# The order of three partial products: low weights last in the dense tiles of a two-block layer, and its first two tiles interleaved

## The reference, cut to what matters

```python
# block one
proj = h @ w_in + b_in                       # 512 x 1024 @ 1024 x 8208
y_a  = spatial_gating(gelu(u), gelu(v))      # u, v: columns of proj
y_b  = gated_delta_rule(silu(conv(qkv)), ...) * silu(z)
merged = sigmoid(gate_a) * (y_a @ w_pa) + sigmoid(gate_b) * (y_b @ w_pb)
h = layer_norm(ALPHA * h + merged @ w_o)
h = layer_norm(ALPHA * h + mixture_of_experts(h))
# block two: input projection (v, k, q, a, x, r, s), attention, recurrence, output projection, feed-forward
```

## Time and profile before

| | us |
|---|---|
| median of 3 runs (lowest, highest) | 2144.96 (2140.62, 2145.87) |
| the profiled execution, its time | 2142.25 |
| the profiled execution, its span | 2140.4 |
| TensorE busy with matmuls | 1981.0 (93% of the span), 9702 matmuls |
| VectorE busy | 926.3 (43%) |
| ScalarE busy | 660.6 (31%) |
| GpSimd busy | 434.7 (20%) |
| TensorE's mean granted clock | 0.969 |

### The profile page before, as it was taken

How to read it: one execution, slowest core, us unless ns; L and a number is a source line. 1 busy time by engine, 2 the same in 40 slices (tenths; PEclk the granted TensorE clock), 3 DMA queues, 4 the chain that set the end, 5 groups by cost and what they waited for, 6 DMA issues and landing times.

```text
span 2140.4 us, 23345 instructions
## 1 busy us (share of the span) xinstructions
PE 1981.0 (93%) x9702; PEld 1447.1 (68%) x9702; DVE 926.3 (43%) x1402; ACT 660.6 (31%) x981; POOL 434.7 (20%) x310
## 2 busy tenths in 40 slices
PE   7999999999999889888788799998889999999999
PEld 6887878888877733333333348777667787888887
DVE  7774376632535622111111145445545883222342
ACT  4554332423333101000000133452137753222221
POOL 5432131423326011111111021311003210000121
PEclk9999999999999889989899999999999999999999
DMA  5861433123244589999999973211111134323210
GB/s 166 273 153 50 99 71 67 40 79 73 53 151 180 199 339 404 407 402 406 412 404 411 424 258 121 87 50 50 50 49 40 39 129 157 118 79 115 83 59 40
DMA packets 99191, 363.14 MB, mean 170 GB/s; under 512 B 10362, under 2 KB 35100, under 8 KB 86792
## 3 DMA queue, kind: packets, MB, share of 16 engines
q1 hardware_dynamic: 88336, 337.24, 44.2%
q0 software_dynamic: 8240, 19.00, 2.6%
q10 hardware_dynamic: 2504, 5.35, 0.7%
HBM read 338.74 MB, written 29.10 MB: 172 GB/s over the span
## 4 chain that ended last, share of the span: by engine, by line
PE 78%; DVE 12%; issue 5%; ACT 5%; DMA 1%; POOL 0%; ACTq 0%; SPq 0%; DVEq 0%; POOLq 0%
PE ps L272 74%; PE ps L276 3%; DVE ST L256 2%; PE ps L2091 2%; DVE H L262 1%; ACT ST L268 1%; DVE WL L256 1%; ACT L268 1%; DVE BG L262 1%; ACT M L268 1%; DVE ST L1005 1%; DVE ML L256 0%; DVE BG L256 0%; DVE H L259 0%; DMA BG<-h1d,toki 0%
## 5 line engine op out<-in xcount | busy, mean ns | idle before, releaser
L272 PE MATMUL ps<-XH,WS 128*128 128x512 f32 x704 | 216.7, 389 | 0.0
L272 PE MATMUL ps<-HTH,WL 128*128 128x512 f32 x448 | 176.4, 394 | 0.0
L272 PE MATMUL ps<-W,BG 128*64 128x512 f32 x496 | 161.8, 621 | 1.0 <-issue 1.0
L272 PEld LDWEIGHTS ps<-XH,WS 128*128 128x128 f32 x704 | 132.2, 188 | 27.3
L2198 DVE COPY BG<-ps 128x512 f32<-128x512 f32 x32 | 22.1, 691 | 288.0 <-PE ps L272 288.0
L266 ACT ACTIVATE BG<-ps 128x512 f32<-128x512 f32 x48 | 28.5, 595 | 376.4 <-PE ps L2091 339.2
L272 PE MATMUL ps<-XL,WS 128*128 128x512 f32 x352 | 137.0, 389 | 1.4 <-DVE XL L256 1.4
L272 PE MATMUL ps<-M,BG 128*64 128x512 f32 (+1 forms) x304 | 123.4, 550 | 6.4 <-ACT ST L266 6.4
L272 PE MATMUL ps<-X2H,GV 128*128 128x512 f32 (+1 forms) x512 | 128.9, 342 | 0.0
L272 PE MATMUL ps<-ST,BG 128*64 128x512 f32 (+2 forms) x416 | 100.4, 586 | 21.9 <-issue 20.5
L272 PE MATMUL ps<-BG 128*64 128x512 f32 (+2 forms) x256 | 93.9, 542 | 20.9 <-issue 20.7
(11 more groups left out here) (396 smaller groups left out, 4428.3 us busy)
## 6 DMA issues: line engine op xcount, KB each, us to landing
W<-in_w SPq DMA_DIRECT2D x31, 2048.0 KB, 39.1
W<-in_w_in SPq DMA_DIRECT2D x27, 2048.0 KB, 10.4
ST<-in_w SPq DMA_DIRECT2D x21, 2048.0 KB, 35.8
BG<-in_w SPq DMA_DIRECT2D x11, 2048.0 KB, 32.8
U<-in_w SPq DMA_DIRECT2D x11, 2048.0 KB, 32.4
M<-in_w SPq DMA_DIRECT2D x11, 2048.0 KB, 36.9
HT<-in_w SPq DMA_DIRECT2D x11, 2048.0 KB, 38.7
W<-in_w_ffn_in SPq DMA_DIRECT2D x22, 1024.0 KB, 7.6
```

What stands on the lines that cost most here:

```text
L272: return p.e.matmul(o, lhsT=l, rhs=r, start=start, stop=stop, skip_group_check=True)
```

## The change

In all dense tiles but the first two, the 24 matmuls of a tile are issued in another order. First come, for all eight steps, the two products that need only the high part of the weights (16 matmuls); then, for all eight steps, the eight products with the low part of the weights. The wait in front of the tile is now for the high part, and the wait for the low part stands between the two passes. The point where the weaving may change over moves from after step 3 to after step 5, which is twelve matmuls into the tile as before. In tiles 24 to 31, in the output projection of block one, in the values, keys and all other tiles of block two's input projection the same order is used. `gr_high` names the wait for a granule's high part; for granules 27 on it is the same wait as for the low part.

Tiles 0 and 1 keep the old order of products, but each is cut after six steps, and `p_qk` issues six steps of tile 0, six of tile 1, two of tile 0, two of tile 1.

```diff
--- before.py
+++ after.py
@@ -654,17 +654,29 @@
         def p_dense(n, bank, rhs, kind, between=()):
             t = B.tile(("d", n), bank, nr=2 if n < 24 else 1)
             room(t)
-            if n == 0:
-                occupy(t, 8)
-            p.wait_ge(*split_done(("d", n)))
             x, hi, lo = parts(("d", n))
-            for k in range(8):
-                p.wait_ge(*split_done((kind, k)))
-                z = exact(t.at, (hi[:, k, :], lo[:, k, :]), (rhs[0][:, k, :], rhs[1][:, k, :]), k == 0, k == 7)
-                if k in between:
-                    p_sum(*between[k])
-                if k == 3:
-                    yield
+            if n < 2:
+                if n == 0:
+                    occupy(t, 8)
+                p.wait_ge(*split_done(("d", n)))
+                for k in range(8):
+                    p.wait_ge(*split_done((kind, k)))
+                    z = exact(t.at, (hi[:, k, :], lo[:, k, :]), (rhs[0][:, k, :], rhs[1][:, k, :]), k == 0, k == 7)
+                    if k == 5:
+                        yield
+            else:
+                p.wait_ge(sp_hi, job["d", n] + 1)
+                for k in range(8):
+                    p.wait_ge(*split_done((kind, k)))
+                    mm(t.at, hi[:, k, :], rhs[1][:, k, :], start=k == 0, stop=False)
+                    mm(t.at, hi[:, k, :], rhs[0][:, k, :], start=False, stop=False)
+                    if k in between:
+                        p_sum(*between[k])
+                    if k == 5:
+                        yield
+                p.wait_ge(*split_done(("d", n)))
+                for k in range(8):
+                    z = mm(t.at, lo[:, k, :], rhs[0][:, k, :], start=False, stop=k == 7)
             z.then_inc(t.filled)
             w_used[n // 4] = [t.full()]
 
@@ -674,10 +686,14 @@
             t = B.tile(("d", n), bank)
             room(t)
             for k in range(8):
+                p.wait_ge(sp_hi, job["v", y, k // 2] + 1)
+                mm(t.at, HTH[:, k, m], hi[:, k, :], start=k == 0, stop=False)
+                mm(t.at, HTL[:, k, m], hi[:, k, :], start=False, stop=False)
+                if k == 5:
+                    yield
+            for k in range(8):
                 p.wait_ge(*split_done(("v", y, k // 2)))
-                z = exact(t.at, (HTH[:, k, m], HTL[:, k, m]), (hi[:, k, :], lo[:, k, :]), k == 0, k == 7)
-                if k == 3:
-                    yield
+                z = mm(t.at, HTH[:, k, m], lo[:, k, :], start=False, stop=k == 7)
             z.then_inc(t.filled)
             w_used[n // 4] = [t.full()]
 
@@ -899,8 +915,11 @@
         SUMS_AFTER = {3: [(0, 0)], 4: [(0, 1)], 5: [(0, 2), (0, 3)], 7: [(1, 0)], 8: [(1, 1)], 9: [(1, 2), (1, 3)]}
 
         def p_qk():
+            first = [p_dense(n, n, hTp, "T") for n in range(2)]
+            for x in first:
+                next(x)
             for n in range(12):
-                for _ in p_dense(n, n % 4, hTp, "T"):
+                for _ in first[n] if n < 2 else p_dense(n, n % 4, hTp, "T"):
                     pass
                 if n == 2:
                     p_ab()
@@ -1651,8 +1670,12 @@
                     room(t)
                     for k in range(8):
                         p.wait_ge(*split_done(("M", k)))
+                        p.wait_ge(sp_hi, job["wo", y, k // 2] + 1)
+                        mm(t.at, MH[:, k, z], hi[:, k, :], start=k == 0, stop=False)
+                        mm(t.at, ML[:, k, z], hi[:, k, :], start=False, stop=False)
+                    for k in range(8):
                         p.wait_ge(*split_done(("wo", y, k // 2)))
-                        i = exact(t.at, (MH[:, k, z], ML[:, k, z]), (hi[:, k, :], lo[:, k, :]), k == 0, k == 7)
+                        i = mm(t.at, MH[:, k, z], lo[:, k, :], start=False, stop=k == 7)
                     i.then_inc(t.filled)
                     w_used[20 + y] = [t.full()]
                     if m and y == 0:
@@ -2618,6 +2641,9 @@
                 return gr_lo[0], (N_GELU + 1) // 2 + 1 + j - N_GELU
             return (gr_lo[1], (j + 1) // 2) if j % 2 else (gr_lo[0], j // 2 + 1)
 
+        def gr_high(j):
+            return (gr_hi, j + 1) if j < N_GELU else gr_low(j)
+
         def gr_in(E, j):
 
             E.wait_ge(*w_ready[gr_src(j)])
@@ -2695,9 +2721,13 @@
             if m == 4:
                 occupy(t, 12)
             x2_ready(m)
+            p.wait_ge(*gr_high(0))
+            for k in range(8):
+                mm(t.at[0:w, 0:256], X2H[:, k, z], o[0][:, k, :], start=k == 0, stop=False)
+                mm(t.at[0:w, 0:256], X2L[:, k, z], o[0][:, k, :], start=False, stop=False)
             p.wait_ge(*gr_low(0))
             for k in range(8):
-                i = exact(t.at[0:w, 0:256], (X2H[:, k, z], X2L[:, k, z]), (o[0][:, k, :], o[1][:, k, :]), k == 0, k == 7)
+                i = mm(t.at[0:w, 0:256], X2H[:, k, z], o[1][:, k, :], start=False, stop=k == 7)
             i.then_inc(t.filled)
             gr_read[0] = t.full()
 
@@ -2705,12 +2735,16 @@
 
             o = gr_buf(1 + n)
             x2_ready(2 * h + 1)
-            p.wait_ge(*gr_low(1 + n))
+            p.wait_ge(*gr_high(1 + n))
             c, z = [(t.at[:, 512 - HALF:512], slice(0, HALF)), (t.at[:, 512:512 + HALF], slice(HALF, NTK))][h]
             if h == 0:
                 room(t)
             for k in range(8):
-                i = exact(c, (o[0][:, k, :], o[1][:, k, :]), (X2H[:, k, z], X2L[:, k, z]), k == 0, k == 7)
+                mm(c, o[0][:, k, :], X2L[:, k, z], start=k == 0, stop=False)
+                mm(c, o[0][:, k, :], X2H[:, k, z], start=False, stop=False)
+            p.wait_ge(*gr_low(1 + n))
+            for k in range(8):
+                i = mm(c, o[1][:, k, :], X2H[:, k, z], start=False, stop=k == 7)
             if h:
                 i.then_inc(t.filled)
                 gr_read[1 + n] = t.full()
@@ -2731,15 +2765,21 @@
             for j, (kind, n) in GRAN3:
                 o = gr_buf(j)
                 if kind == "x":
-                    p.wait_ge(*gr_low(j))
+                    p.wait_ge(*gr_high(j))
                     b = pairs.pop(0)
                     t = B.tile((kind, n), b, wide=True)
                     room(t)
+                    sides = ((t.at[:, 512 - HALF:512], slice(0, HALF)), (t.at[:, 512:512 + HALF], slice(HALF, NTK)))
                     for k in range(8):
-                        for c, z in ((t.at[:, 512 - HALF:512], slice(0, HALF)), (t.at[:, 512:512 + HALF], slice(HALF, NTK))):
-                            i = exact(c, (o[0][:, k, :], o[1][:, k, :]), (X2H[:, k, z], X2L[:, k, z]), k == 0, k == 7)
-                        if k == 3:
+                        for c, z in sides:
+                            mm(c, o[0][:, k, :], X2L[:, k, z], start=k == 0, stop=False)
+                            mm(c, o[0][:, k, :], X2H[:, k, z], start=False, stop=False)
+                        if k == 5:
                             yield
+                    p.wait_ge(*gr_low(j))
+                    for k in range(8):
+                        for c, z in sides:
+                            i = mm(c, o[1][:, k, :], X2H[:, k, z], start=False, stop=k == 7)
                     i.then_inc(t.filled)
                     pairs.append(b)
                     f.wide = b
@@ -2752,11 +2792,15 @@
                     room(t)
                     if (kind, n) in (("r", 6), ("s", 5)):
                         occupy(t, 8)
+                    p.wait_ge(*gr_high(j))
+                    for k in range(8):
+                        mm(t.at, o[0][:, k, :], X2L[:, k, NMETA:NTK], start=k == 0, stop=False)
+                        mm(t.at, o[0][:, k, :], X2H[:, k, NMETA:NTK], start=False, stop=False)
+                        if k == 5:
+                            yield
                     p.wait_ge(*gr_low(j))
                     for k in range(8):
-                        i = exact(t.at, (o[0][:, k, :], o[1][:, k, :]), (X2H[:, k, NMETA:NTK], X2L[:, k, NMETA:NTK]), k == 0, k == 7)
-                        if k == 3:
-                            yield
+                        i = mm(t.at, o[1][:, k, :], X2H[:, k, NMETA:NTK], start=False, stop=k == 7)
                     i.then_inc(t.filled)
                     singles.append(b)
                     gr_read[j] = t.full()
```

## The result

| | before | after |
|---|---|---|
| median of 18 runs each, on one chip | 2142.61 us | 2147.48 us |
| lowest, highest | 2136.68, 2148.78 | 2144.60, 2149.07 |
| ratio of times (95% interval) | | 1.0021 (1.0013, 1.0030) |
| profiled execution, its span | 2140.4 us | 2143.9 us |

The change makes the kernel 0.2% slower, some 4.5 us. I had forecast −0.1 us. Most of the forecast's steps came out nearly to the number; one place, which I had not priced, took more than all the others together.

What follows compares the result with a forecast made beforehand. TensorE was taken to bound the kernel (78% of the chain), except the DMA-bound expert stage. Terms −0.5 − 1.1 + 1.2 + 0.3 gave −0.1 us, 2144.8 us against the 2144.96 us median; range 2138.5 to 2150.8 us.

Steps and rivals of the forecast that it cites:

- start: Tiles 0 and 1 interleaved: TensorE restarts near 27.9 us instead of 28.38 us, and the gain is kept: −0.5 us.
- sums in tile 18: The first sum's 0.18 us bank wait grows by 0.45 us, swallowed by TensorE's 4.54 us wait at 169.17 us: 0.
- woven tiles: Waits of 0.57 and 0.56 us at 310.28 and 435.43 us go; those at 293.94 and 428.02 us bring 0: −1.1 us.
- tile 72: First tile on gated V: new waits for steps 6 and 7; tile 73 begins at 639.3 us, not 638.10: +1.2 us.
- output projection: First tile: the 1.00 us wait for low weights goes, 1.3 us of work comes in its place: +0.3 us.
- block two: Second block: waits for banks, input pieces and weights that VectorE splits stay as they are: 0.
- slower rival: Half-speed clock behind thinned work at 637 and 687 us: +3.1 us (2148 us), or +8 us (2153 us); chance 0.17.
- rival that the waits only move: Saved woven waits reappear at the next turn, the start's 0.5 us in a VectorE chain: +1.5 us, 2146.5 us; chance 0.12.

Runs made afterwards that it cites:

- b_tile22: The kernel before with the new order in tile 22 alone; measured ratio 1.0009 (0.9995, 1.0023).
- best3: The changed kernel with tiles 22, 72 and the output projection's first tile in the old order, tile 18 new; ratios 0.9981 and, repeated, 0.9984.
- best1: The changed kernel with tiles 18, 22, 72 and the output projection's first tile in the old order; ratios 0.9998 and, repeated, 0.9985.

## Why the forecast was wrong, step by step

| step | forecast | drift in the change's profile | |
|---|---|---|---|
| start | −0.5 | −0.5 at the place itself, −0.3 by 160 us | right in this profile; the times can't tell |
| sums in tile 18 | 0 | −2.2 (160 to 180) | see below |
| sums in tile 22 | not priced | **+4.8** (200 to 240) | the step that failed |
| woven tiles | −1.1 | −0.4; −2.0 without the clock at 311.5 us | won more than forecast |
| tile 72 | +1.2 | +1.1 | size right, one wait for two |
| output projection | +0.3 | +0.3 | right |
| block two | 0 | 0 | right |

**The failed step** is "Column sums in tile 18". I priced the sums' move by the wait for their bank alone. That wait was right: 0.18 + 0.45 = 0.63 us was worked out and 0.63 us is what the profile shows. But I took only the tile where before had a stall and did not ask what else the packing does, and tile 22, with the same sums in it and no slack behind, was not priced at all. What the runs show in its place is 6.8 and 3.4 us at a granted clock of 0.50 behind tile 22, +4.8 us. My slower rival had the mechanism, a fall of the clock where the change thins out TensorE's work, and put it at 637 and 687 us, "at exactly two places". There the clock costs nothing new: one stretch of 3.4 us at 0.5 in the output projection, as before, and one that ends at 635.7 us, ahead of tile 72's last pieces, which is 6.8 us long where before's was 3.4, but just as long in the profile of the interleaved start alone. What I held against this rival, that the 2.07 us wait at 28.38 us had no such stretch behind it, was the chance of one execution: in the profile of b_tile22, whose start is that of before, one of 3.4 us begins at 30.4 us. The third place, full of small matmuls, I had not listed because nothing waits there. That this rival's +3.1 us agrees with the +3.2 us of the three measurements is luck: it was added up from two other places.

**Tile 18.** Packed in the same way, it also has the clock fall (near 158 us), but ahead of the 4.54 us wait of the earlier trace rows, which swallows it; and the stretch at half clock that before has from 168.2 us, behind this wait, is gone, which is 2.2 us won in the profile. The profile of the interleaved start alone, with old sums, shows a like −2.8 us. The step of 2.1 to 2.4 us between 160 and 180 us comes back in all ten profiles with tile 18's sums packed, but in the timed runs tile 18 alone is +0.06% and best3 no better than best1 in one group. That it shortens the whole program is not shown.

**Woven tiles.** The waits of the earlier trace rows are gone, and the first was worth nothing, as said: the turn behind it waits 1.24 us where it had waited 0.70 us. At 310.28 and 435.43 us 0.8 us each were won in most profiles and not 0.57 (at 310 us in 8 of the 11 with the new order in these tiles, at 435 us in all), and another 0.3 us by 600 us, which I can't place. In three profiles, the change's own among them, the longer wait at that turn is followed by 3.4 us at half clock (311.5 us above), which gives 1.6 us back. The rival that the waits only move thus came true in part, but by way of the clock, which it had not named.

**Start, tile 72, output projection.** TensorE restarted at 27.87 us (27.9 forecast), held by GpSimd's split of tile 1; VectorE's first convolution came at 35.08 us (35) and took 4.35 us, so nothing late came of it. From 30 to 42 us TensorE's own drift falls by 0.5 us in the change's profile. In tile 72 I had forecast two waits of 0.4 and 1.0 us; there is one of 0.71 us, since a half-clock stretch ahead of it delays TensorE into the pieces; the loss is the same. In the output projection the wait for the low weights went and 8 matmuls came behind the last piece: +0.3.

**Does it add up?** Start −0.5, woven −2.0, and −1.3 at the output projection where its first tile stays old: −3.8 us for best1, measured −1.8 over its two measurements. The change itself: −0.5 − 2.0 + 1.1 + 0.3 + 4.8 = +3.7, measured +3.2 over three measurements (+4.5 in the first). This sum leaves out the 2.2 us that tile 18 won in the profile, since no timed run shows them, and the 1.6 us of the clock at 311.5 us, which came in three profiles only; with tile 18's it is +1.5, so what becomes of that gain later in the program stays open. What is left is about as large as the intervals of some ±2 us, so the agreement proves no single term. In a single profile it need not add up: from 760 us on, stretches at half clock come and go (before has them at 1342, 1503 and 1578 us, the change at 1503, 1520 and 1684 us), and the profiles of one kernel end up to 4.8 us apart (the change 2140.6, 2143.9 and 2145.0, best3 2135.3 and 2140.1).

My range in absolute time, 2138.5 to 2150.8 us, held the measured 2147.48, and the rise of 0.21% lies within the 0.3% that I had counted as no change with a chance of 0.81. What did not hold is the forecast itself, −0.1 us and within 2 us of before (0.58): the rise is +4.5 us, and its interval of some 0.09% to either side, from 18 runs of each, leaves no room for none. That 0.3% is the least that can be told here was also wrong.

## What to carry to other kernels

When an edit regroups matmuls, list every place rich in small matmuls (few columns) that the edit touches, and carry half of a half-clock stretch for each as a risk, also where TensorE never waits and nothing else is late. Which arrangement is spared could not be told here in advance. A reordering that moves work off a wait is good where the weights are late and bad where the streamed input is: there the moved products were the filler between pieces, so keep the old order for the one or two tiles behind such an input. Compare such small changes by drift against several profiles of each kernel, since a single one can hold 4 to 5 us of chance.

## What was not expected of the hardware

The granted clock fell to 0.50 at 202.3 us although TensorE had issued matmuls without a gap for over 6 us; of the last 5 us, 3.2 us were sums of one column per matmul. The same program text (best3 and its repeat) ran the 10.1 us from 202.1 us with 72 matmuls at 1.00 in one execution and with 39 at 0.50 in the other. What exactly decides is open: the spread order lost as much as the packed one. Nor did the fall always cost: ahead of a wait for VectorE (157.9 us) it was free, and the next one, which before has at 168.2 us, did not come.
